# Differential attention in a hybrid decoder layer: the squares of the head outputs, taken per token tile in place of per tile and head

## The reference, cut to what matters

```python
def diff_attention(q, k, v, cos, sin, lam, subln_w, lambda_init):
    ...                                   # 4 heads, 2 softmaxes of 64 dims each, v of 128 dims
        p = jax.nn.softmax(s, axis=-1)    # causal
        attn = p[:, :, 0] - lam * p[:, :, 1]
        return jnp.einsum('bhqk,bhkv->bhqv', attn.astype(v.dtype), v)
    o = lax.map(block, jnp.arange(L // Q_BLOCK))
    o = o.transpose(1, 0, 3, 2, 4).reshape(Bsz, L, DIFF_HEADS, 2 * DIFF_HEAD_DIM)
    o = rms_norm(o, subln_w) * (1.0 - lambda_init)   # mean of squares over 128 values, per token and head
```

## Time and profile before

| | |
|---|---|
| time, median of 3 runs | 1505.02 us (1504.80 to 1506.93) |
| profiled execution | 1507.82 us, its span 1506.1 us |
| PE busy | 1452.8 us (96%) |
| DVE busy | 947.6 us (63%) |
| ACT busy | 691.4 us (46%) |
| POOL busy | 80.1 us (5%) |
| attention loop | about 343 to 458 us of the span |

### The profile page before, as it was taken

One profiled execution on the slowest core, in us unless ns is written; L12 is line 12 of the kernel. 1 busy time (PEld: TensorE's weight loads), 2 busy tenths in 40 slices (PEclk: granted clock), 3 DMA queues, 4 the chain that ended last, 5 costly groups with the idle time before them and its releaser, 6 DMA issues.

```text
span 1506.1 us, 22980 instructions
## 1 busy us (share of the span) xinstructions
PE 1452.8 (96%) x8724; PEld 1267.3 (84%) x8724; DVE 947.6 (63%) x1656; ACT 691.4 (46%) x1479; POOL 80.1 (5%) x132
## 2 busy tenths in 40 slices
PE   7999999998989999999999989999999999999998
PEld 5889999995669999787999968888888788888886
DVE  5783566637885425512632688887777575557798
ACT  6324222337885424523732566445444464444443
POOL 1000000000010001100000252000000000000012
PEclk9999999998999999999999999999999999999999
DMA  8112111111003610111011332665443598676563
GB/s 319 57 31 57 29 29 29 43 43 57 1 1 113 236 45 29 56 43 42 2 46 47 114 130 73 227 201 185 154 147 126 204 334 293 233 231 195 157 232 126
DMA packets 99436, 177.66 MB, mean 118 GB/s; under 512 B 9600, under 2 KB 42496, under 8 KB 97280
## 3 DMA queue, kind: packets, MB, share of 16 engines
q1 hardware_dynamic: 93632, 152.05, 29.8%
q10 hardware_dynamic: 5696, 24.15, 5.0%
HBM read 138.42 MB, written 37.75 MB: 117 GB/s over the span
## 4 chain that ended last, share of the span: by engine, by line
PE 64%; DVE 3%; ACT 2%; issue 2%; POOL 0%; DMA 0%; POOLq 0%; DVEq 0%; ACTq 0%
PE ps L2043 20%; PE ps L2045 20%; PE ps L2044 20%; PE ps L2340 2%; PE ps L2087 1%; PE ps L2354 0%; DVE opl L1627 0%; POOL rms L706 0%; DVE wq_l L1786 0%; DMA raw<-in_w_mk_dram 0%; DVE mix L1583 0%; DVE resid L1659 0%; DVE wl L1285 0%; PE ps L2223 0%; PE ps L2242 0%
## 5 line engine op out<-in xcount | busy, mean ns | idle before, releaser
L2043 PE MATMUL ps<-wh,oph 128*128 128x256 f32 (+1 forms) x1024 | 293.4, 286 | 3.2 <-issue 1.7
L2044 PE MATMUL ps<-wl,oph 128*128 128x256 f32 (+1 forms) x1024 | 289.0, 282 | 0.0
L2045 PE MATMUL ps<-wh,opl 128*128 128x256 f32 (+1 forms) x1024 | 288.9, 282 | 0.0
L2043 PEld LDWEIGHTS ps<-wh,oph 128*128 128x128 f32 x1024 | 194.2, 190 | 4.2 <-issue 2.2
L2044 PEld LDWEIGHTS ps<-wl,oph 128*128 128x128 f32 x1024 | 194.4, 190 | 0.1
L2045 PEld LDWEIGHTS ps<-wh,opl 128*128 128x128 f32 x1024 | 194.2, 190 | 0.0
L2043 PE MATMUL ps<-d_ring 128*128 128x512 f32 x448 | 175.3, 391 | 2.1 <-DVE d_ring L1917 2.1
L2045 PE MATMUL ps<-d_ring 128*128 128x512 f32 x448 | 175.1, 391 | 0.0
L2044 PE MATMUL ps<-d_ring 128*128 128x512 f32 x448 | 174.9, 390 | 0.0
L1285 DVE TENSOR_TENSOR wl<-raw,wh 128x1024 fp32r<-128x1024 f32 (+1 forms) x60 | 73.2, 1224 | 93.3 <-ACT wh L767 92.5
L706 POOL TENSOR_TENSOR rms<-stat,mhalf 128x1 f32<-128x1 f32 (+2 forms) x59 | 44.5, 762 | 1382.0 <-DVE stat L1289 1360.6
(11 more groups left out here) (348 smaller groups left out, 2945.0 us busy)
## 6 DMA issues: line engine op xcount, KB each, us to landing
right_raw<-in_w_down_dram SPq DMA_DIRECT2D x128, 256.0 KB, 3.9
u_kept_s<-us SPq DMA_DIRECT2D x64, 256.0 KB, 3.4
left_raw<-u_kept_s SPq DMA_DIRECT2D x64, 256.0 KB, 2.8
w_blk<-in_w_up_blocks_dram ACTq DMA_DIRECT2D x14, 1024.0 KB, 5.8
left_raw<-u_kept_a SPq DMA_DIRECT2D x48, 256.0 KB, 3.1
raw<-in_w_in_dram SPq DMA_DIRECT2D x18, 512.0 KB, 3.8
u_kept_a<-u SPq DMA_DIRECT2D x24, 256.0 KB, 2.2
x_in<-in_x_dram SPq DMA_DIRECT2D x8, 512.0 KB, 8.6
```

Source lines behind the costliest of these rows:

```text
L2043: te.matmul(o, lh, rh, start=first, stop=False)
L2044: te.matmul(o, lh, rl, start=False, stop=False)
L2045: return te.matmul(o, ll, rh, start=False, stop=last)
```

## The change

The square per step is taken out; the output copy (L965) now signals `o_ev`. In its place ScalarE gets one `o_square` per completed token tile: it waits until its own copy of the last head has been written, reads the four heads' outputs of the tile from SBUF (128 x 4 x 128) and writes 512 squares into one of two halves of `junk`. VectorE adds them up with one `tensor_reduce` to four columns, waits for that to be written, and goes on with the mean as before. In ACT's turn n the new square comes after `probs_evac` part 1 and ahead of the exponentials.

```diff
+        o_sq, o_sums = sem("o_sq"), sem("o_sums")
...
+            def o_square(k):
+
+                i = O_COMPLETE[k]
+                m = MIX_TILES.index(i)
+                act.wait_ge(o_ev, k + 1)
+                if m == 0:
+                    act.wait_ge(sq_done, 2 * NT)
+                if m >= 2:
+                    act.wait_ge(o_sums, m - 1)
+                s.activation(junk[:, 512 * (m % 2):512 * (m % 2) + 512].rearrange("p (h c) -> p h c", h=DH), mix[:, 4:8, i * P:(i + 1) * P],
+                             ACT.Square).then_inc(o_sq, 1)
...
-                    s.activation(mix[:, 4 + h, i * P:(i + 1) * P], o, ACT.Copy, scale=recs[:, k % 4, 0:1])
-                    if k >= 4:
-                        act.wait_ge(o_ev, k - 3)
-                    elif k == 0:
-                        act.wait_ge(sq_done, 2 * NT)
-                    s.activation(junk[:, (k % 4) * P:(k % 4 + 1) * P], o, ACT.Square, scale=recs[:, k % 4, 0:1],
-                                 accum_out=stat[:, COL[("o", i)] + h:COL[("o", i)] + h + 1]).then_inc(o_ev, 1)
+                    s.activation(mix[:, 4 + h, i * P:(i + 1) * P], o, ACT.Copy, scale=recs[:, k % 4, 0:1]).then_inc(o_ev, 1)
                 if n >= 2 and n - 2 < NS and steps[n - 2][0] >= 4:
                     probs_evac(n - 2, 1)
+                if n - 3 in O_COMPLETE:
+                    o_square(n - 3)
                 if n < NS:
                     attn_exp(n, 0)
                     attn_exp(n, 1)
...
             def o_mean(i):
-                dve.wait_ge(o_ev, O_STEP[i] + 1)
+                m = MIX_TILES.index(i)
+                dve.wait_ge(o_sq, m + 1)
+                c = stat[:, COL[("o", i)]:COL[("o", i)] + DH]
+                v.tensor_reduce(c, junk[:, 512 * (m % 2):512 * (m % 2) + 512].rearrange("p (h c) -> p h c", h=DH), AX.X, ALU.add).then_inc(o_sums, 1)
+                dve.wait_ge(o_sums, m + 1)
                 mean(("o", i), P, DH)
```

## The result

The changed kernel takes 1512.53 us (median of 4 runs, 1511.35 to 1512.99), the kernel before beside it 1504.91 (4 runs, 1504.71 to 1506.93). The ratio is 1.0045, with a 95% interval from 1.0032 to 1.0058: slower by 4.8 to 8.7 us. The forecast was 1509.6, in a range from 1503.5 to 1513.5. The profiled execution took 1512.58 with a span of 1510.8, 4.7 more than the span before.

A forecast was written before the change was run, and what follows sets the result against it. No engine in the loop has room to spare (PE, DVE, ACT 18.8, 17.1, 17.2 of 20 us), so edits were placed turn by turn: 2.13 + 1.42 + 1.06 = 4.61 us later, from 1505.02 to 1509.6, range 1503.5 to 1513.5.

The forecast's parts named there:

- Even turns: Attention loop, removed squares: evacuation part 1 waits for PE's transposes anyway, so no gain, except 0.1 us in turn 18.
- Turn 7: Attention loop: ACT is late there with the memory squares too, so removing the square gains 0.19 us.
- Turn 18: Attention loop, tile 2: new square delays both exponentials, for which DVE waits; 0.53 less 0.11, so 0.42 us later.
- Turn 26: Attention loop, tile 1: new square ahead of the exponentials shows in full, 0.53 us later.
- Turn 33: Tile 4: memory evacuation stands right behind the new square and DVE's low part waits for it; 0.30 us later.
- turns 9, 10, 17, 25: Attention loop, tiles 7, 3, 6, 5: new squares fit into ACT's idle time ahead of exponentials or evacuation; cost nothing.
- Turns 12, 20, 28: Attention loop: VectorE's sum of 0.71 us fits where DVE idles 0.85 to 0.97 us for an exponential; costs nothing.
- Turns 13, 21, 29: Attention loop: sums behind o_norm's four multiplications, with DVE busy afterwards, show in full; 3 x 0.71 = 2.13 us later.
- The last two: Turns 36 and 37: sums in the serial chain of DVE and POOL ahead of the weights' low parts; 1.42 us later.
- Relief pays: Rival: ScalarE sets the pace in every turn, so the kernel gets 3.2 us faster, 1501.8; chance 0.10.
- Only the tail pays: Rival: the loop's delays shift into idle times, only 1.42 + 0.30 us is left, 1506.7; chance 0.20.
- Everything shows: Third rival: hidden sums and squares don't fit in, 9.0 us, 1514.0, or the reduction takes 1.13; chance 0.12.

The follow-up runs named there:

- the change with the late square: Changed kernel with the square per tile behind the two exponentials in ScalarE's turn instead of ahead of them; 1510.40 us, ratio 1.0034.
- the squares per tile: Changed kernel without VectorE's sums: squares per tile on ScalarE, means read a constant; 1506.85 us, ratio 1.0006 to the kernel before.
- the norms moved in the change: Changed kernel with the square per tile behind the exponentials and o_norm moved to later places; 1505.78 us, ratio 0.9988 to the kernel before.
- the norms moved in the kernel before: Kernel before with o_norm moved: five to turns 15, 17, 23, 25, 31, one to 33, two behind the last mean; 1504.39 us, ratio 0.9979.

## Why the prediction was right, point by point

**The order of reading.** ACT had 17.16 of 20 us of work, and taking it down to 15.29 gave nothing. The step from busy shares to single turns was the one that mattered: 32 x 0.36 was counted as 0.2, and the run without the squares shows 0.08 between turns 10 and 30.

**Removed.** Even turns: nothing, by the 0.44 us of waiting in turn 16. Turn 7: 0.19 expected. From the evacuation at 373.86 to that at 377.29 the kernel before takes 3.43, the one after 3.24 (374.28 to 377.52), so 0.19. But between the evacuations of turns 3 and 9, which start at 356.81 and 381.21 before and at 357.28 and 381.37 after, it is 24.40 and 24.09, so 0.31; between the same two the second profile of the kernel before takes 23.28 and the change with the late square 22.99, both at full clock there. The 0.12 over it comes beside turn 7, 0.05 from turn 6 to 7 and 0.07 from turn 8 to 9; turns 4 and 6, which I had written off because PE has no gap there, gave nothing. A small miss.

**ScalarE's squares.** Turn 18: 0.42 expected, 0.43 measured. Turn 26: 0.53 and 0.50. Turn 33: 0.30 and 0.32. The turns 9, 10, 17, 25 nothing, as expected.

**VectorE's sums.** 0.68 expected and 0.676 measured, 0.72 with the wait in place of 0.71. Turns 12, 20, 28 nothing: in turn 12 the reciprocal waits 0.16 where it waited 0.88, so the cover was used up almost to the end:

```profile
395.26 0.67 DVE L1588 TENSOR_REDUCE stat<-junk 128x4 f32<-128x512 f32 x1
396.76 0.17 DVE L1578 RECIPROCAL recs<-sums 128x2 f32<-128x2 f32 x1 [0.16 <-ACT probs L934]
```

Turns 13, 21, 29: 2.13 expected, 0.73 + 0.73 + 0.74 = 2.20 measured. The last two: 1.42, measured 1.44. The sum of the edits is 2.20 + 1.44 + 0.43 + 0.50 + 0.32 - 0.31 = 4.58, where 4.61 was predicted. The Trainium skill's VectorE: DVE Perf Modes, The TRN2 errata, would by its fixed cycles, as an estimate, have had the sum 65 ns below one from PSUM. It measured 676 ns for 684 after and 682 before, a tenth of that.

**What was missing.** The delay at `wl` is 6.35 us, 1.8 more than 4.58. 0.27 of it was there before the loop began (its first scores start at 341.01 for 340.74), 0.2 comes in the fall at 345 to 360, which both profiled executions have and which lay a little worse in this one. 1.30 is left, and it lies between the evacuations of turns 31 and 33 (2.88 + 2.92 us for 2.42 + 2.08), in the fall in 450 to 460. PE's part of that, the same ten matmuls of the product with v, before and after:

```profile
449.29 1.29 PE L2258 MATMUL ps<-vt,probs_t 128*128 128x128 f32 x10
```

```profile
452.66 2.34 PE L2271 MATMUL ps<-vt,probs_t 128*128 128x128 f32 x10
```

The sum had no term for the clock. I had read 1.00 in the loop and carried it over to a kernel in which PE waits more. With 1.3 the same working gives 5.9 and 1510.9. The 1.3 isn't a price that holds elsewhere: with the squares left out the end is 2.6 longer with a fall of the same length, and with the squares per tile a shorter one, behind the last evacuation, cost nothing.

**Span and median.** Behind `wl` the delay stays at 6.3 until 1186 us; then the kernel before loses 1.6 by a fall of its own (0.93 in 1175 to 1200), so the spans differ by 4.7 only. That one execution of each differ by about my sum is therefore partly luck. The column of the lost clock says the same: of the kernel before, 6.0 us more of it (10.4 against a mean of 4.4) come with 5.35 us more span, 0.89 each. Taking that off, and for the fall in 450 to 460 its 1.3, leaves 1496.8 for the three profiles of before (1506.1 - 9.3, 1501.0 - 3.7, 1500.5 - 4.1, on average) and 1501.3 for those of the change (1510.8 - 7.7 - 1.3, 1510.9 - 8.9 - 1.3, 1512.1 - 9.3 - 1.3): 4.5 apart. That it is just the sum of the edits is luck, as the 0.89 hangs on three profiles: a line through the 68 timed executions of the kernel before gives 0.70 us for each us lost, and with that the same working ends 5.2 apart. The timed executions test the sum in another way. At the same mean granted clock those of the change are longer by 3.3 us (0.990), 4.0 (0.991) and 3.4 (0.992), 16 of them against 27 of the kernel before. 4.6 + 1.3, less the 2.4 that a loss of 3.4 us costs on average, would be 3.5. The timed ratios of 1.0040 to 1.0045 are 6.0 to 6.8 us, nearer to 4.6 + 1.3.

**The range.** 1512.53 lies above the forecast's own range of 1507.8 to 1511.8. (The bounds that I had worked out, 3.5 and 7.1 later, are 1508.5 and 1512.1; the measured time is above these too.) It is inside 1503.5 to 1513.5 because the upper end was drawn out for the third rival, whose reason turned out wrong. So the step from edits to turns was right and that the time is inside the wide range is in part luck: what filled it was mostly the clock, for which I had no term.

**The rivals.** Relief pays: refuted, by the kernel without squares. Only the tail pays: refuted, as each of the three sums behind a norm shows in full. Everything shows: its 1514.0 is nearer to the result than my 1509.6, but its reason is refuted, since turns 9, 10, 12, 17, 20, 25 and 28 took their work for nothing; the clock makes up the difference.

**Left open.** What brings the clock down in 450 to 460. It comes with the change in three profiles of three, but also with the squares left out, where the loop is no longer and DVE has nothing added; it stays away with the norms moved in the change and comes, in part, with the norms moved in the kernel before. PE was as idle in 450 to 453 before, with no fall behind it. Fall and cost are shown, and over the timed executions the change loses 3.0 us more clock than the kernel before. By what step the added waits bring that about is not shown; it can be a matter of how PE's idle time happens to lie.

## What to carry to other kernels

Work taken off an engine is worth what its next instruction gains in start time, turn by turn; look at what releases that instruction, and if it is another engine, the relief becomes a wait. An accumulator output that rides on an operation in a covered place is cheap; before trading it for a pass of another engine, look whether that pass stands ahead of something for which two engines wait, and whether it can stand elsewhere. Ask the same of what is there already: moving the norm took 1.8 us off the loop. Time short sections by marks that the edit doesn't move, and look for the clock in them first. And when a change gives PE new idle time, put a term for the clock into the sum and into the range.

## What the runs showed of the hardware

- TensorE's granted clock falls to its lower level, 1.2 GHz, for some microseconds behind places where PE is partly idle, but not behind every such place, and the same kernel has it in some executions and not in others: three profiles of the kernel before have 10.4, 4.2 and 4.6 us of lost clock, and spans of 1506.1, 1501.0 and 1500.5. Its timed executions in the later comparisons spread from 1502.6 to 1511.9.
- What a fall costs depends on what stands in it: at the end of the loop 1.3 us in the change and about 2.6 with the squares left out, with 3.4 us of lost clock in both; nothing with 1.7 in the squares per tile, where it lies behind the last evacuation.
- A reduction of 128x512 takes the same from SBUF (676 ns) as from PSUM (684), with four outputs as with one.
- Two kernels whose loops differ by 0.9 us (before, and with the squares per tile) couldn't be told apart in 24 and 12 runs, while the distance between two marks of the loop, at full clock, repeats to 0.02 us.
